# Score products in one order by shape, a third copy on ScalarE at the first change of tile, and eight buffers for modulation bias rows

## The chip, the cores and the metric

The kernel runs on one core of one Trainium2 chip. Its time is the device time of one execution in microseconds, as the median of a few runs. In the profile PE is the TensorE matmul, PEld its weight loads, DVE VectorE, ACT ScalarE, POOL GpSimd and SP SyncE; the DMA engines move data between memory (HBM) and the on-chip SBUF. Matmuls write into PSUM, which has eight banks of 512 float32 per partition.

## The reference

A trunk of two layers over 256 latent tokens and 256 context tokens, width 1024, all in float32. Each layer normalises, modulates, mixes, adds, and is followed by PEER, a mixer that picks 16 experts per head for each token:

```python
mod_x = split(silu(c) @ w_mod[i] + b_mod[i], 6)          # and mod_c from c_ctx
hx = rms_norm(x, norm1[i]) * (1 + mod_x[1]) + mod_x[0]
# layer 0: gated short convolution + bidirectional gated DeltaNet, layer 1: latent attention
x = x + mod_x[2] * mixer(hx)
hx2 = rms_norm(x, norm2[i]) * (1 + mod_x[4]) + mod_x[3]
x = x + mod_x[5] * peer(hx2)

def peer(hb):                  # for a tile of 128 tokens, 8 heads, 16 experts each
    s1, i1 = top_k(scores of half 0); s2, i2 = top_k(scores of half 1)
    sc, idx = top 16 of all sums s1 + s2
    gate = softmax(sc)
    act = gelu(einsum('td,thkd->thk', hb, u_tab[idx]))
    return einsum('thk,thkd->td', gate * act, v_tab[idx])

def attention(q, k, v):        # 8 heads, q and k are 128 plain + 64 rotary columns
    return softmax(q @ k.T * scale) @ v
```

## The kernel before

The program is written engine by engine: each engine has its own list of instructions in a fixed order, written out by hand, and waits for semaphores of the others. It has four blocks.

**First block (`first_block`, L1890).** The 24 chunks of modulation (2 layers, 12 chunks of 512 columns each) are computed by PE from 2 MB of weights each that SP loads (`mod_pe`, L1841). Chunks 0 to 3 come at the start, chunks 4 to 23 one after another inside the DeltaNet mixer of the context tokens, woven with its stages by `beside`. For chunk n DVE adds the bias (`mod_dve`, L1854), which POOL has loaded into `mod_row[n % 4]`, and for gains it multiplies with `norm_row[n % 4]`. The rows lie in `straight` (1024 columns, 128 for each) and `diag`, both unused by anything else in this block. POOL stores the result to memory, waits until the store before it has landed, and loads the bias of chunk n + 3 (loop at L1928). DVE's instructions of the mixer stand behind `mod_dve` in its order. In a mixer chunk PE computes KS, vT, QS, kT, then vnew, intraV and dS, and DVE takes them at L1130, L1135 and L1139, L1143, L1146, L1153, L1163, L1170 and L1173; then ACT squares the output (L977), and output product, norm, scores and ranking follow up to the first gather.

**Sums (`sums_and_mixer`, L2716; `last_sums`, L3228).** There are six tiles of 128 tokens (T_ 0 to 5, 8 heads each, head number G = 8 T_ + h). For each expert k of a head POOL gathers 128 rows of 8 KB (1 MB) into one of 9 slots (L2063), DVE forms the dot products with the first half (L2267), ACT makes gelu, coefficient and a diagonal matrix `diag` of two experts (L2079, L2080, L2085), and PE adds the second halves with eight 64x64 products (16 matmul records) into four banks of PSUM (L2185), which frees the two slots for POOL's next two gathers. Two of the four banks hold sums in place (straight), two hold the halves of partitions crossed over. Between these groups of two experts the rest of the kernel is woven in by stages; in tiles 0 and 1 that is the whole context-free half of layer 0 (its projections and mixer), with the same lines as in the first block. Where one tile ends, ACT copies the crossed halves into the tile's place (L2114), DVE adds the straight ones during the next head, after its fourth dot product (`SUM_AT`, L2120), and the place then holds the sum. Tiles 0 and 1 use the same four banks. PE waits before its first group of tile 1 (`tile_open_pe`, L2150) through

```python
        def sums_copied(pe, T_):
            pe.wait_ge(peer_crossed, 2 * T_ + 2)      # ACT's two copies
            pe.wait_ge(peer_straight, T_ + 1)         # DVE's add
```

**The pause (`second_block`, L2833).** After tile 3 no gather can run: the attention of layer 1 needs the last context tile. Attention of the latent tile 2 over the first three tiles of keys was computed earlier; here the scores against the last 128 keys (`st`, two banks, one for even and one for odd heads) are merged with it. PE's order is: keys; scores (L2994 with 128 rows, L2995 with 64 rotary rows, `rows_of(par)`); values (L2490, recorded at L1246); the turned probabilities (L3003); the rest of a projection (L1246); new outputs (L3013); turns (L3020); the output product (L1246). DVE takes each bank's maximum (L2921 to L2924), copies half of the values (`values_take`, L2926), rescales the earlier output (L2930 to L2934) and adds the new (L2938). ACT takes the exponentials (L2881, four for each bank), then the other half of the values (L2885).

A float32 product shows as two matmul records; a turn (a product with the identity) as one.

## Time and profile before

| | |
|---|---|
| median of 3 runs | 2475.72 us (2472.72 to 2481.14) |
| the profiled execution | 2469.39 us, its span 2467.6 us |
| mean granted TensorE clock | 0.859 of 2.4 GHz |
| PE, PEld busy | 1776.8 us (72%), 847.2 us (34%) |
| DVE, ACT, POOL busy | 1630.6 us (66%), 971.8 us (39%), 980.0 us (40%) |
| DMA | 938.60 MB, mean 380 GB/s |

The span goes from the first instruction to the last; 1.8 us of the profiled execution's time lie around it. All times in the rows are from the span's start. Busy shares are means over stages with different limits, so they do not tell what an edit is worth; the chain of waits does, which is followed back from the last instruction, at each step to what released it. In it "issue" is time in which an engine waited for nothing that the profile shows. In a timeline row the bracket gives the idle time before and who ended it; "x16" is the number of records merged in the row.

### The profile page before, as it was taken

The numbers are of one execution on the slowest core, as the hardware profiler recorded it, in microseconds if no ns is written. First come the engines' busy times: TensorE is split into PE (matmuls) and PEld (weight loads), VectorE is DVE, ScalarE is ACT, GpSimd is POOL, SyncE is SP. The second block draws the span as 40 slices with busy tenths as digits, with TensorE's granted clock in tenths as the row PEclk, the third lists the DMA queues.
The fourth block names the chain that finished last, engine by engine and source line by source line (L and its number), as shares of the span: only waits on it lengthen the run. The fifth ranks groups of instructions, "written<-read, shape, count | busy, mean of one in ns | idle before, by whom it ended". The sixth has DMA issues, their size and how long they took to land.

```text
span 2467.6 us, 35626 instructions
## 1 busy us (share of the span) xinstructions
PE 1776.8 (72%) x13118; PEld 847.2 (34%) x13118; DVE 1630.6 (66%) x3826; ACT 971.8 (39%) x2654; POOL 980.0 (40%) x896
## 2 busy tenths in 40 slices
PE   7998979997875869557665566766978765555555
PEld 5877656553542215112221122221643411111111
DVE  1544567969997676577666675775386666666665
ACT  3411147744434334235533353453254333433333
POOL 3014133344443334445544444443044444454452
PEclk9999999998998889768787887888998968787877
DMA  8278689999989999999999999998389999999997
GB/s 353 75 274 343 256 332 385 421 421 421 382 360 423 420 422 404 418 422 421 422 421 421 420 415 420 409 405 340 147 369 421 420 421 421 418 421 421 420 419 293
DMA packets 127967, 938.60 MB, mean 380 GB/s; under 512 B 17168, under 2 KB 18192, under 8 KB 20784
## 3 DMA queue, kind: packets, MB, share of 16 engines
q0 software_dynamic: 114800, 807.34, 79.3%
q1 hardware_dynamic: 12992, 128.97, 13.0%
q8 instruction: 104, 1.70, 0.3%
q14 instruction: 71, 0.58, 0.1%
HBM read 935.10 MB, written 1.15 MB: 379 GB/s over the span
## 4 chain that ended last, share of the span: by engine, by line
DMA 42%; PE 34%; DVE 11%; ACT 6%; issue 6%; POOL 1%; DVEq 0%; SPq 0%; ACTq 0%; POOLq 0%
DMA arena<-in_experts,expert_cur 37%; PE ps L2185 13%; PE ps L1246 12%; DVE arena L2267 5%; DMA last_slot<-in_experts,expert_cur 4%; ACT diag L2085 2%; PE ps L1850 2%; PE ps L1271 2%; PE ps L1258 1%; PE ps L1482 1%; ACT coef L2080 1%; PE ps L1463 1%; ACT acts L2079 1%; POOL arena L2063 1%; ACT L2079 1%
## 5 line engine op out<-in xcount | busy, mean ns | idle before, releaser
L2185 PE MATMUL ps<-arena,diag 64*64 64x512 f32 x5464 | 980.9, 767 | 554.8 <-ACT diag L2085 548.5
L2063 POOL DMA_INDIRECT arena<-in_experts,expert_cur x683 | 811.0, 1187 | 1142.5 <-PE ps L2185 909.5
L2267 DVE CUSTOM_DVE_ANT_0 arena<-arena 128x1024 f32<-128x1024 f32 x683 | 838.6, 1229 | 510.6 <-DMA arena<-in_experts,expert_cur 498.0
L2185 PEld LDWEIGHTS ps<-arena,diag 64*64 64x64 f32 x5464 | 237.3, 158 | 1126.9 <-ACT diag L2085 800.7
L2079 ACT ACTIVATE acts<-dots 128x2 f32<-128x2 f32 (+1 forms) x386 | 78.6, 204 | 1007.6 <-DVE dots L2267 993.3
L2085 ACT ACTIVATE diag<-consts,coef 128x128 f32<-128x128 f32 x768 | 266.4, 393 | 12.6
L2185 PE MATMUL ps<-last_slot,diag 64*64 64x512 f32 x680 | 211.4, 749 | 45.2 <-ACT diag L2085 45.1
L2080 ACT ACTIVATE coef<-acts,gate_cur 128x1 f32<-128x1 f32 x768 | 185.1, 288 | 12.6
L1246 PE MATMUL ps<-wring 128*128 128x256 f32 (+2 forms) x568 | 146.7, 410 | 0.0
L2267 DVE CUSTOM_DVE_ANT_0 last_slot<-last_slot,arena 128x1024 f32<-128x1024 f32 x85 | 104.4, 1228 | 55.0 <-DMA last_slot<-in_experts,expert_cur 53.6
L2063 POOL DMA_INDIRECT last_slot<-in_experts,expert_cur x85 | 100.6, 1183 | 92.2 <-PE ps L2185 77.0
L1246 PEld LDWEIGHTS ps<-wring 128*128 128x128 f32 x568 | 100.6, 197 | 63.6 <-issue 54.8
L1246 PE MATMUL ps<-arena,wring 128*128 128x256 f32 (+1 forms) x576 | 115.1, 357 | 0.1
L1246 PEld LDWEIGHTS ps<-arena,wring 128*128 128x128 f32 x576 | 98.9, 194 | 19.3 <-issue 8.2
L2079 ACT ACT_TABLE_LOAD x80 | 102.6, 1283 | 6.7 <-DVE dots L2267 5.3
L1869 POOL DMA_DIRECT2D mods<-straight x48 | 26.7, 558 | 166.7 <-DVEq L1864 159.3
L2185 PEld LDWEIGHTS ps<-last_slot,diag 64*64 64x64 f32 x680 | 51.2, 160 | 110.5 <-ACT diag L2085 72.5
L2267 DVE DVE_READ_ACCUMULATOR2_ANT dots<- 128x1 f32 x768 | 63.1, 82 | 0.0
L2091 ACT ACT_TABLE_LOAD x47 | 60.3, 1283 | 0.8
L1850 PE MATMUL ps<-wring,small 128*2 128x128 f32 x1152 | 38.3, 282 | 16.0 <-DMA wring<-in_w_mod 11.8
L1246 PE MATMUL ps<-arena 128*128 128x128 f32 (+2 forms) x190 | 44.8, 390 | 2.0 <-ACT arena L2469 0.8
L1258 PE MATMUL ps<-arena 128*128 128x128 f32 x352 | 45.0, 281 | 1.7 <-issue 1.7
(402 smaller groups left out, 1985.5 us busy)
## 6 DMA issues: line engine op xcount, KB each, us to landing
wring<-in_w_mod SPq DMA_DIRECT2D x18, 2048.0 KB, 9.8
wring<-in_ev_w_in SPq DMA_DIRECT2D x14, 1024.0 KB
arena<-in_w_mod SPq DMA_DIRECT2D x6, 2048.0 KB, 10.0
wring<-in_ev_w_in SPq DMA_DIRECT2D x6, 2048.0 KB, 13.9
arena<-in_experts,expert_cur POOLq DMA_INDIRECT x683
wring<-in_w_q SPq DMA_DIRECT2D x5, 2048.0 KB, 12.8
wring<-in_ev_w_out SPq DMA_DIRECT2D x3, 2048.0 KB, 12.6
arena<-in_ev_w_in SPq DMA_DIRECT2D x1, 2048.0 KB, 19.9
```

Of the source, the lines that this page charges most:

```text
L1246: ins = nc.tensor.matmul(dst, l, r, start=first and i == 0, stop=last and i == len(pairs) - 1)
L1258: last = (M(dst, lhsT(h), rhs(h), start=True, stop=True) if op is M else TR(dst, lhsT(h), rhs(h)))
L1271: last = M(dst, lhsT[c, u, :], rhs[c, u, :], start=True, stop=plus is None)
L1850: last = nc.tensor.matmul(ps[32 * g:32 * g + 2, 6 + n % 2, 0:P], sT[:, 2 * k:2 * k + 2], w[:, k, g, :], start=(k == 0), stop=(k == KT - 1))
L1869: pool.dma_start(quarters(mods[i, s, c // 2, (c % 2) * 512:(c % 2) * 512 + 512]), mod_row[n % 4][s:P:32]).then_inc(rows_stored[n % 2], 16)
L2063: nc.gpsimd.indirect_dma_start(ring_slot(slot), None, table, bass.IndirectOffsetOnAxis(ap=expert_cur[:, par, k:k + 1], axis=0),).then_inc( ...
L2079: act_step(nc.scalar.activation(acts[:, par, g], dots[:, par, g], ACT.Gelu))
L2080: act_step(*[nc.scalar.activation(coef[:, par, k:k + 1], acts[:, par, k:k + 1], ACT.Copy, scale=gate_cur[:, par, k:k + 1]) for k in ks])
L2085: nc.scalar.activation(diag[:, k % RING, :], const(IDENT), ACT.Copy, scale=coef[:, par, k:k + 1]).then_inc(diag_ready, 1)
L2091: nc.scalar.activation(gate_exp[:, :], best[:, :], ACT.Exp, bias=gate_stat[:, 0:1], accum_out=gate_stat[:, 1:2]).then_inc(gexp_ready, 1)
L2185: last = nc.tensor.matmul(ps[rows_of(o), sum_bank(G // PH, odd, c), :], diag[rows_of(i), k % RING, rows_of(i)], ring_slot(RING_SLOT[G, k]) ...
L2267: ins = nc.vector.tensor_tensor_reduce(out=ring_slot(slot)[:, 0:D], in0=ring_slot(slot)[:, 0:D], in1=place, scale=1.0, scalar=0.0, op0=ALU ...
```

## The change

Three edits. (1) `mod_row` and `norm_row` get eight entries instead of four. Four more stretches of `straight` and `diag` are zeroed, and the rows of chunks 4 to 7 are loaded behind the small constants, before the first store; the loop then loads chunk n + 7 after storing chunk n. (2) At the end of tile 0 alone, ACT also copies the straight sums, into `straight`; PE waits for ACT's three copies and no more for DVE, and DVE adds `straight` from SBUF. (3) In the pause, PE does the eight score products over 128 rows first, then the eight over 64 rows, alternating between the even and the odd bank and with that between the two halves of rows; DVE's copy of its half of the values moves behind the four small steps of the first bank.

```diff
+ROWS = 8
...
-        mod_row = [straight[:, P * k:P * k + P] for k in range(4)]
-        norm_row = [diag[:, k, :] for k in range(4)]
+        mod_row = [straight[:, P * k:P * k + P] for k in range(ROWS)]
+        norm_row = [diag[:, k, :] for k in range(ROWS)]
...
+        first_sums_kept = sem("first_tile_sums_copied")
...
         def mod_dve(dve, n):
             V = nc.vector
-            dve.wait_ge(row_landed[n % 4], 32 * sum(1 + is_gain(m) for m in range(n % 4, n + 1, 4)))
+            dve.wait_ge(row_landed[n % ROWS], 32 * sum(1 + is_gain(m) for m in range(n % ROWS, n + 1, ROWS)))
...
+                nc.gpsimd.memset(straight[:, N_COLUMNS * P:ROWS * P], 0.0).then_inc(rows_zero, 1)
+                nc.gpsimd.memset(diag[:, N_COLUMNS:ROWS, :], 0.0).then_inc(rows_zero, 1)
+                pool.wait_ge(rows_zero, 4)
+                for n in range(N_COLUMNS, ROWS):
+                    load_mod_rows(pool, n)
...
-                    if n and n + 3 < len(MODS):
+                    if n and n + ROWS - 1 < len(MODS):
                         if n <= N_COLUMNS:
                             pool.wait_ge(column_done, n)
-                        load_mod_rows(pool, n + 3)
+                        load_mod_rows(pool, n + ROWS - 1)
...
             for i in range(2):
                 nc.scalar.copy(by_banks(place)[rows_of(i)], crossed_sum(T_, i)).then_inc(peer_crossed, 1)
+            if T_ == 0:
+                nc.scalar.copy(by_banks(straight[:, :]), straight_sum(T_)).then_inc(first_sums_kept, 1)
...
             dve.wait_ge(peer_crossed, 2 * T_ + 2)
-            nc.vector.tensor_tensor(by_banks(place), by_banks(place), straight_sum(T_), ALU.add).then_inc(peer_straight, 1)
+            if T_ == 0:
+                dve.wait_ge(first_sums_kept, 1)
+                nc.vector.tensor_tensor(place, place, straight[:, :], ALU.add).then_inc(peer_straight, 1)
+            else:
+                nc.vector.tensor_tensor(by_banks(place), by_banks(place), straight_sum(T_), ALU.add).then_inc(peer_straight, 1)
...
             else:
-                sums_copied(pe, T_ - 1)
+                pe.wait_ge(peer_crossed, 2)
+                pe.wait_ge(first_sums_kept, 1)
...
-                values_take(dve, V.tensor_copy, 3, 1)
                 for par, c in enumerate(parity):
...
                     step(V.tensor_tensor(alpha_rec[:, c], alpha[:, c], all_rec[:, c], ALU.mult))
+                    if par == 0:
+                        values_take(dve, V.tensor_copy, 3, 1)
                     step(V.tensor_tensor(half_o[:, par], half_o[:, par], over(alpha_rec[:, c]), ALU.mult))
...
                 for par in range(2):
                     for i in range(4):
-                        at = slice(i * P, (i + 1) * P)
-                        M(banks[par][:, at], qnT[2][:, 2 * i + par, :], knT[:, 2 * i + par, new], start=True, stop=False)
-                        last = M(banks[par][:, at], qrT[2][rows_of(par), i, :], krT[rows_of(par), new], start=False, stop=True)
-                    product.mark(last, ("st", par))
+                        M(banks[par][:, quarter(i)], qnT[2][:, 2 * i + par, :], knT[:, 2 * i + par, new], start=i == 0,
+                          stop=False, skip_group_check=True)
+                for i in range(4):
+                    for par in range(2):
+                        last = M(banks[par][:, quarter(i)], qrT[2][rows_of(par), i, :], krT[rows_of(par), new], start=False,
+                                 stop=True, skip_group_check=True)
+                        if i == 3:
+                            product.mark(last, ("st", par))
```

## Rows read from the trace of the kernel before

**Rows 1.** The page: the chain that ended last, by engine.

```profile
DMA 42%; PE 34%; DVE 11%; ACT 6%; issue 6%; POOL 1%; DVEq 0%; SPq 0%; ACTq 0%; POOLq 0%
```

**Rows 2.** The chain of waits in the first block, 235 to 345 us: start, duration, what.

```profile
252.35 7.72 DMA mods<-straight
...
261.17 7.20 DMA straight<-in_b_mod
```

**Rows 3.** Timeline, 236 to 300 us: start, duration, engine, line, names, count, [idle before].

```profile
266.93 1.49 PE L1258 MATMUL ps<-arena 128*128 128x128 f32 x11 [0.86 <-issue]
...
268.40 0.29 DVE L1859 TENSOR_TENSOR straight<-ps,straight 128x128 f32<-128x128 f32 x1 [2.77 <-DMA straight<-in_b_mod]
...
269.13 5.65 PE L1258 MATMUL ps<-arena 128*128 128x128 f32 x48
...
273.17 1.29 DVE L1163 TENSOR_TENSOR arena<-arena,ps 128x512 f32<-128x512 f32 x2 [0.21 <-PE ps L1258]
...
275.82 1.28 DVE L1173 TENSOR_TENSOR arena<-arena,ps 128x512 f32<-128x512 f32 x2
```

**Rows 4.** Timeline of POOL alone, 0 to 64 us.

```profile
16.15 1.16 POOL L1869 DMA_DIRECT2D mods<-straight  x2 [4.16 <-DVEq L1864]
```

**Rows 5.** Timeline, 690 to 720 us, the first change of tile.

```profile
700.07 2.04 ACT L2114 COPY arena<-ps 64x1024 f32<-64x1024 f32 x2 [4.73 <-PE ps L2185]
...
702.88 0.69 ACT L2085 ACTIVATE diag<-consts,coef 128x128 f32<-128x128 f32 x2
...
707.89 1.15 DVE L2120 TENSOR_TENSOR arena<-arena,ps 128x1024 f32<-128x1024 f32 x1
...
709.14 3.69 PE L2185 MATMUL ps<-arena,diag 64*64 64x512 f32 x16 [4.00 <-issue]
...
713.12 0.94 POOL L2063 DMA_INDIRECT arena<-in_experts,expert_cur  x1 [10.64 <-PE ps L2185]
...
714.23 0.69 DVE L1163 TENSOR_TENSOR wring<-wring,ps 128x512 f32<-128x512 f32 x1 [1.33 <-PE ps L1258]
```

**Rows 6.** Stretches: PE, PEld, DVE, ACT, POOL busy us; granted clock; DMA share; GB/s.

```profile
706.00:722.00 16.00, 12.86 (x142) 7.82 (x143) 13.15 (x24) 5.93 (x15) 4.50 (x4) 0.79 0.60 222
708.00:714.00 6.00, 4.86 (x25) 2.12 (x26) 4.80 (x7) 4.66 (x11) 0.88 (x1) 0.56 0.22 89
720.00:731.00 11.00, 9.28 (x102) 5.94 (x96) 10.50 (x28) 5.28 (x18) 8.87 (x8) 1.00 0.89 324
731.00:750.00 19.00, 13.41 (x96) 5.92 (x96) 16.59 (x41) 4.62 (x18) 9.11 (x8) 0.91 1.01 423
```

**Rows 7.** Timeline of PE alone, 700 to 760 us.

```profile
723.28 1.95 PE L2185 MATMUL ps<-arena,diag 64*64 64x512 f32 x16 [0.22 <-ACT diag L2085]
```

**Rows 8.** Timeline, 1725 to 1790 us, the pause between the two layers' sums.

```profile
1735.67 3.84 PE L1246 MATMUL ps<-arena 128*128 128x128 f32 x32 [0.76 <-ACT arena L2469]
...
1740.81 0.46 PE L2994 MATMUL ps<-arena 128*128 128x128 f32 x2
...
1741.20 0.49 PE L2995 MATMUL ps<-late,arena 64*128 64x128 f32 x2
...
1745.47 0.37 ACT L2881 ACTIVATE arena<-ps,small 128x128 f32<-128x128 f32 x1 [7.12 <-DVEq L2925]
...
1747.45 3.70 PE L1246 MATMUL ps<-arena 128*128 128x512 f32 x8
...
1751.86 1.46 PE L1246 MATMUL ps<-wring,straight 128*128 128x384 f32 x4
...
1753.15 1.95 PE L3013 MATMUL ps<-x,arena 128*128 128x128 f32 x16
...
1754.85 2.16 DVE L2938 SCALAR_TENSOR_TENSOR arena<-ps,small,arena 128x128 f32<-128x128 f32 x8
```

**Rows 9.** Timeline, 1778 to 1830 us: products over 64 rows.

```profile
1784.06 0.72 PE L3067 MATMUL ps<-arena,consts 64*128 64x128 f32 x8 [0.51 <-issue]
...
1790.87 1.13 PE L2788 MATMUL ps<-late 64*128 64x512 f32 x4
```

More of the change, by code:

```diff
@@ L577, in build @@
         c_landed = sem("c_landed")
-        row_landed = [sem(f"mod_bias_landed{i}") for i in range(4)]
+        row_landed = [sem(f"mod_bias_landed{i}") for i in range(ROWS)]
         mod_done = sem("mod_chunk_done")
@@ L1855, in mod_dve @@
             V = nc.vector
-            dve.wait_ge(row_landed[n % 4], 32 * sum(1 + is_gain(m) for m in range(n % 4, n + 1, 4)))
+            dve.wait_ge(row_landed[n % ROWS], 32 * sum(1 + is_gain(m) for m in range(n % ROWS, n + 1, ROWS)))
             dve.wait_ge(mod_done, n + 1)
-            row = mod_row[n % 4]
+            row = mod_row[n % ROWS]
             V.tensor_tensor(row, ps[:, 6 + n % 2, 0:P], row, ALU.add).then_inc(mod_taken, 1)
@@ L1861, in mod_dve @@
             if is_gain(n):
-                dve_step(V.scalar_tensor_tensor(out=row, in0=row, scalar=1.0, in1=norm_row[n % 4], op0=ALU.add,
+                dve_step(V.scalar_tensor_tensor(out=row, in0=row, scalar=1.0, in1=norm_row[n % ROWS], op0=ALU.add,
                                                 op1=ALU.mult))
@@ L1869, in store_mod_rows @@
                 pool.dma_start(quarters(mods[i, s, c // 2, (c % 2) * 512:(c % 2) * 512 + 512]),
[L1870 removed]
+                               mod_row[n % ROWS][s:P:32]).then_inc(rows_stored[n % 2], 16)
         def column_pe(pe, n):
@@ L1919, in _ @@
                 pool.wait_ge(rows_zero, 2)
-                for n in range(4):
+                for n in range(N_COLUMNS):
                     load_mod_rows(pool, n)
```

10 lines of the change are left out of this document (5 added, 5 removed).

## The prediction

> **What bounds the kernel now.** I read the page first, then the chain of waits, then timelines of the three places that the change touches, then the table of stretches for the DMA engines. Over the whole span the chain is DMA 42% and PE 34% [rows 1]: the experts' rows come from memory at one rate for long stretches, and the waits between them are short pieces where another engine ends last. So an edit is worth what it takes out of one of those pieces, and I read each piece by itself. Three matter.
>
> First, the end of the first block. The chain passes through a store of modulation rows that takes 7.72 us to land and a load of bias rows of 7.20 us, one behind the other on POOL's queue [rows 2]; DVE stands 2.77 us for the last row's bias (L1859, 268.40) [rows 3]. Second, the first change of tile, near 705 us. ACT copies the crossed sums at 700.07 to 702.11 (L2114), but DVE comes to its add (L2120) only at 707.89, and PE, which must wait for both before it opens tile 1 in the same banks, stands idle 4.00 us until 709.14 [rows 5]. Its group then takes 3.69 us, and only then does POOL issue the next gather, at 713.12, having waited 10.64 us. Meanwhile the DMA engines run dry: their share is 0.60 over 706 to 722 us and 0.22 over 708 to 714, where the granted clock is 0.56, that is, mostly the lower of its two levels [rows 6]. From 731 us their share is 1.01. Third, the pause between the two layers' sums, 1720 to 1795 us, where no gather is in flight and PE, ACT and DVE follow each other in one serial chain.
>
> **Part 1, eight bias rows.** The last row's load (n = 23) is issued today when the store of row 19 has landed; with eight buffers it is issued at n = 16, seven chunks ahead, so DVE's 2.77 us goes. What is late next: DVE's L1143 needs the state product QS, whose matmuls PE does at 266.93 to 268.42 [rows 3], and PE does not wait for DVE there. Step by step: DVE does row 23 by 265.95, takes the first half of QS at 267.4 and the second at 268.45, ends at 269.1 (1.0 us ahead of now), then L1146 and L1153 at their own 1.28 and 1.4 us to 271.9. L1163 needs intraV; PE's 48 matmuls from 269.13 take 5.65 us whatever DVE does, and intraV is their second third, done about 272.9. The second L1163 then ends at 273.7, the two L1170 at 275.1 and L1173 at 276.4, against 275.82 + 1.28 = 277.10. So 2.77 us of wait are worth 0.7 us. Bounds: 0, if PE's own order holds all of it; 1.6, if PE's pause of 0.86 us inside QS goes too. All behind it (squares, output product, ranking, first gather) is serial, so 0.7 us stays. The costs: two more memsets and eight more loads on POOL, about 8 x 0.56 + 1.0 = 5.5 us, in a hole of 4.16 us before the first store [rows 4]; that store goes 1.4 us later and nobody waits for it (the columns are turned on PE from SBUF, and what it frees is loaded for a chunk that comes more than 100 us later). Without that cover it would be at most 5.5 us. I take 0.
>
> **Part 2, ACT copies the straight sums too, at the first change only.** ACT's third copy writes 128x1024; the copies of 64x1024 take 1.0 us each [rows 5] and time goes by elements per partition, so 1.05 us, to 703.15. ACT's queue behind it: gelu, coefficients and the diagonals of head 8, which end now at 703.57, then at 704.6; two copies of vnew, later by 1.0 but needed by PE only after its group. PE finishes the woven work at 709.14 - 4.00 = 705.14, later than all of these, so it opens tile 1 at 705.2: 3.9 us earlier. It has not stood idle, so I take its group at 1.95 us, as the group at 723.28 [rows 7] in a stretch whose granted clock is 1.00, that is 2.4 GHz [rows 6], not 3.69. The slots are free at 707.15 and POOL issues at 707.4 instead of 713.12: 5.7 us earlier. The next pair of slots is freed after PE's woven intraV and level products (4 us), at about 713 instead of 718.9, the pair after that when DVE's dots and ACT allow, at 716.5. So the DMA engines, with two gathers of 1 MB at 2.5 us each, stay fed: of the 16 x (1 - 0.60) = 6.4 us idle in 706 to 722 about 2 remain, 4.4 gained.
>
> DVE sets the other limit. Its add still stands at 707.89, both operands in SBUF now, at the same price; so DVE gains only its waits for PE, 1.33 us at 714.23 and some 0.6 at the two level products behind it, 2.0 in all. In 731 to 750 us DVE is busy 16.59 of 19 us [rows 6], so it can catch up 2.4 us more as its data comes sooner: 4.4 again. From there DMA's share is 1.01, which keeps what it has gained. I take 4.4. Bounds: 2.0 (DVE never catches up, and the gathers queue behind it) and 5.7 (the whole advance of the first gather); 0 is excluded as long as PE's 4.00 us goes.
>
> **Part 3, the pause's scores.** Now 8 products over 128 rows and 8 over 64 alternate, each two matmul records, from 1740.81 to 1747.45: 6.64 us for 32 records, 0.21 each. The key products just before have the same 128x128 shape at the same clock and take 3.84 us for 32, 0.12 each [rows 8]. So the alternation costs almost as much again. After: 16 records at 0.12 make 1.9 us. For the 64-row ones the two nearest rows are 0.72 us for 8 records, which are not alternated between row halves, and 1.13 us for 4 of 512 columns, which are [rows 9]; the first gives 1.4 us for 16 records, the second, at a quarter of the columns, 1.13. I take 1.4: 3.3 us in all, 3.3 less. If a change of row half cost as much as a change of shape does now, they would stay at 0.21: 3.4 us, and the gain would be 1.4. The Trainium skill, "TensorEngine Tiling (Array Packing)", section Key Properties, says that a change of tiling mode, not of tile alone, drains the engine. By that rule the alternation is what costs, and the new order, with one change instead of fifteen, keeps the 3.3 us; the trace agrees that the alternation is dear, 0.21 against 0.12, and cannot show the rest, as no row has 128-column products that change row half.
>
> What is late next: st 1 is now ready at 1744.1, not 1747.5, but st 0 too, and it was ready at 1744.2 before; so ACT's first four exponentials begin at 1745.4 as now (1745.47) [rows 8] and take about 1.6 us. The second four follow at once, at 1747.1, and end at 1748.7. PE does the two value products meanwhile, 3.70 us to 1747.8, turns the probabilities by 1749.05, does the rest of the query latent (1.46) to 1750.5 and the new outputs (1.95) to 1752.4. DVE's values copy, moved behind the first half's four small steps, fills a time in which it waits for the second alpha; in its old place it would hold the first half behind the value product, so moving it costs nothing and keeps DVE ahead of PE: both half_o multiplications end by 1750.9. L2938 (eight, 2.16 us) starts at 1751.5, is held once by PE, and ends at 1753.7 instead of 1757.01. The output product, which waits for it, then starts 3.3 us earlier, and that is kept whole, since what follows to the first gather is serial. Its last weights are asked for at 1750.5 and first needed some 5 us later. Bounds: 1.0 (ACT's second set is the only thing that moves) and 3.9.
>
> **The sum.** 0.7 + 4.4 + 3.3 = 8.4 us, with bounds 3.0 and 11.2. The profiled execution took 2469.39 us, the span 2467.6 and 1.8 around it; it would be 2461.0. The median of the runs shown is 6.3 us above it, so for the median I say 2475.7 - 8.4 = 2467.3. A measurement here can tell about 0.3%, 7.4 us, from no change, so the forecast lies just beyond that line.
>
> **The rivals.** (a) DVE keeps the tile change's gain down. For it: DVE is busy 10.50 of 11 us in 720 to 731 [rows 6], and its own gain there is only 2.0 us; against it, 2.4 us are free in the 19 us behind. Then 0.7 + 2.0 + 3.3 = 6.0 us, 2469.7. (b) The 64-row products remain slow because they alternate row halves; the chain then gains 1.4 us instead of 3.3: 6.5 us in all, 2469.2. For it: nothing in the trace has 128-column products alternating so; against: the pair of 512 columns overlaps, 1.13 us for what two such would take alone. (c) The refill of 705 us does not count: DMA was only early, and later holes are as long. Then 4.0 us, 2471.7; against it is the share of 1.01 behind. (d) Slower: the earlier gathers change which woven products meet which head, PE stands idle longer before some groups, and those run at the lower clock, 3.69 us instead of 1.95 [rows 5, 7], 1.7 us each on the chain. Five such groups cancel the gain; ten make the kernel slower by more than 0.3%, 2484. For it, groups at the lower clock occur all over the sums; against, the DMA queue is full there and hides them. (e) The row buffers do nothing, because PE holds DVE anyway: 7.7 us, 2468.0.
>
> **How the numbers follow.** Forecast, with (e), 0.56; (a) 0.18; (b) 0.10; (c) 0.10; (d) 0.06. The forecast's own range is 2464 to 2470. The range for 8 in 10 leaves out most of (d) and the far end where all bounds are met together: from 2475.7 - 11.2, taken on to 2462 because the three runs shown differ by 8.4 us and their median is loose by a few, up to 2475. More than 0.3% faster (below 2468.3): 0.75 of the forecast case, 0.42, and 0.06 from (a) and (b): 0.48. Slower by more than 0.3%: half of (d) and a little for what I don't see, 0.05. The rest, 0.47, within 0.3%.
>
> **What would show it.** In the profile after: no wait for the bias rows on DVE in the first block, the squares (L977) 0.7 us earlier; PE's group at 705.2 less what came before, at 1.95 us, DMA share over the 16 us behind it near 0.9, and the same lead still there at 800 us; score products in 3.3 us, the output product 3.3 us earlier against the pause's start. I am wrong if PE's pause at 705 is only moved to another wait, if the lead at 800 us is under 3 us, if the 64-row products take 0.2 us each, or if stretches between the three places change length by more than a microsecond or two.

## The result, and the profile after

The changed kernel takes 2463.0 us (median of 6 executions, 2457.4 to 2467.3), the kernel before 2474.8 us (6 executions beside them, 2472.7 to 2481.1). The ratio is 0.9948, with an interval of 0.9932 to 0.9964: 12.9 us faster, 8.9 to 16.8. The forecast was 2467.3 us and a gain of 8.4 us. The direction was right, and the predicted gain is just outside the interval. One execution each of pause_halves, no_rows, tile_waits, tile_twice and rows_twice, 2538 to 8531 us long, is left out of all that follows.

The profiled execution took 2467.28 us, 2.1 us less than that of before and the longest of its six. So the two profiles set side by side hide most of the gain, and each stretch has to be read by its own length, not by its place on the clock.

**The first block.** The timeline of the changed kernel, 262 to 290 us, answers to [rows 3]:

```profile
269.48 1.93 PE L1852 MATMUL ps<-wring,small 128*2 128x128 f32 x64
...
271.34 0.82 PE L1260 MATMUL ps<-arena 128*128 128x128 f32 x5
...
271.63 0.28 DVE L1861 TENSOR_TENSOR straight<-ps,straight 128x128 f32<-128x128 f32 x1
...
273.29 1.49 PE L1260 MATMUL ps<-arena 128*128 128x128 f32 x11 [1.13 <-issue]
...
273.93 0.69 DVE L1145 TENSOR_TENSOR arena<-ps,small 128x512 f32<-128x512 f32 x1 [2.01 <-PE ps L1260]
...
281.51 1.29 DVE L1175 TENSOR_TENSOR arena<-arena,ps 128x512 f32<-128x512 f32 x2
```

The last bias row (L1861, which was L1859) no longer waits for anything. The next instruction, L1145, waits 2.01 us in its place, for PE's product QS, and PE itself pauses 1.13 us in the middle of that product with no wait recorded. The wait has changed its name and kept most of its length. PE's products for the last chunk start here at 269.48, and in the kernel before at

```profile
263.39 1.93 PE L1850 MATMUL ps<-wring,small 128*2 128x128 f32 x64
```

From there DVE needs 12.03 us to its last step of the mixer (L1175) where it needed 12.43 (L1173), so 0.4 us is gained on this piece, and PE comes to it 6.1 us later.

**The first change of tile.** The timeline of the changed kernel, 698 to 730 us, answers to [rows 5]:

```profile
707.10 2.04 ACT L2121 COPY arena<-ps 64x1024 f32<-64x1024 f32 x2 [4.69 <-PE ps L2199]
...
709.16 1.01 ACT L2123 COPY straight<-ps 128x1024 f32<-128x1024 f32 x1
...
712.02 1.91 PE L2199 MATMUL ps<-arena,diag 64*64 64x512 f32 x14
...
714.22 0.94 POOL L2070 DMA_INDIRECT arena<-in_experts,expert_cur  x1 [4.67 <-PE ps L2199]
...
714.96 1.15 DVE L2131 TENSOR_TENSOR arena<-arena,straight 128x1024 f32<-128x1024 f32 x1
```

ACT's third copy takes 1.01 us. PE opens the second tile at 711.91 without an idle gap, its 16 products take 2.0 us instead of 3.69, and DVE's add comes only after them. POOL waits 4.67 us for its slot instead of 10.64. The stretches of the changed kernel, with the columns of [rows 6]:

```profile
706.00:722.00 16.00, 12.11 (x179) 8.16 (x174) 14.84 (x27) 11.49 (x25) 6.05 (x6) 1.00 1.02 402
708.00:714.00 6.00, 4.96 (x65) 3.62 (x66) 5.19 (x10) 4.86 (x11) 1.24 (x2) 1.00 1.00 416
713.00:729.00 16.00, 12.03 (x163) 7.65 (x158) 15.07 (x29) 7.43 (x21) 6.17 (x6) 1.00 0.99 384
731.00:750.00 19.00, 13.71 (x104) 6.63 (x96) 18.57 (x49) 5.46 (x20) 10.65 (x10) 0.91 0.98 392
```

ACT's copies start 7.0 us later here than in the kernel before (707.10 and 700.07), so the stretch that answers to its 706 to 722 us is 713 to 729. The DMA engines' share there is 0.99 where it was 0.60, and the granted clock is 1.00 from 706 to 729 us, where 708 to 714 us of the kernel before had 0.56.

**The pause.** The timeline of the changed kernel, 1740 to 1760 us, answers to [rows 8]:

```profile
1742.82 2.02 PE L3009 MATMUL ps<-arena 128*128 128x128 f32 x16
1744.77 1.16 PE L3013 MATMUL ps<-late,arena 64*128 64x128 f32 x16
1745.86 3.70 PE L1248 MATMUL ps<-arena 128*128 128x512 f32 x8
...
1747.21 0.37 ACT L2895 ACTIVATE arena<-ps,small 128x128 f32<-128x128 f32 x1 [6.85 <-DVEq L2939]
...
1750.75 1.46 PE L1248 MATMUL ps<-wring,straight 128*128 128x384 f32 x4
...
1753.21 2.16 DVE L2953 SCALAR_TENSOR_TENSOR arena<-ps,small,arena 128x128 f32<-128x128 f32 x8 [0.68 <-PE ps L3033]
...
1755.92 4.53 PE L1248 MATMUL ps<-wring,arena 128*128 128x512 f32 x10
```

The 32 records of the scores take 1745.86 - 1742.82 = 3.04 us instead of 6.64. The output product, the last row, starts 13.10 us after the first score; in the kernel before that was 16.84 us.

### The profile page after: what moved, and what is told of

Read it like the earlier page. It is cut to its first block, busy times and chain, and to the rows that moved or that the text cites. A ratio compares the mean times of both kernels' runs of the same rounds, so it can differ in the third digit from the quotient of the medians.

```text
span 2465.5 us, 35630 instructions
## 1 busy us (share of the span) xinstructions
PE 1780.7 (72%) x13118; PEld 850.7 (35%) x13118; DVE 1631.1 (66%) x3826; ACT 972.8 (39%) x2655; POOL 966.9 (39%) x898
## 3 DMA queue, kind: packets, MB, share of 16 engines
q1 hardware_dynamic: 12992, 128.97, 13.2%
## 4 chain that ended last, share of the span: by engine, by line
DMA 41%; PE 36%; DVE 11%; issue 6%; ACT 5%; POOL 0%; DVEq 0%; SPq 0%; POOLq 0%; ACTq 0%
DMA arena<-in_experts,expert_cur 36%; PE ps L2199 13%; PE ps L1248 12%; DMA last_slot<-in_experts,expert_cur 4%; DVE arena L2281 4%; ACT diag L2092 2%; PE ps L1852 2%; PE ps L1260 2%; PE ps L1273 2%; PE ps L1484 1%; ACT coef L2087 1%; PE ps L1465 1%; ACT acts L2086 1%; PE ps L1890 1%; DVE last_slot L2281 0%
## 5 line engine op out<-in xcount | busy, mean ns | idle before, releaser
L2070 POOL DMA_INDIRECT arena<-in_experts,expert_cur x683 | 793.2, 1161 | 1144.0 <-PE ps L2199 913.6
L2087 ACT ACTIVATE coef<-acts,gate_cur 128x1 f32<-128x1 f32 x768 | 185.1, 288 | 12.6
L1852 PE MATMUL ps<-wring,small 128*2 128x128 f32 x1152 | 38.1, 281 | 16.1 <-DMA wring<-in_w_mod 11.7
L1248 PE MATMUL ps<-wring,arena 128*128 128x512 f32 x102 | 45.6, 599 | 0.0
## 6 DMA issues: line engine op xcount, KB each, us to landing
arena<-in_w_mod SPq DMA_DIRECT2D x6, 2048.0 KB, 10.4
```

The costliest lines, as they stand in the source:

```text
L1248: ins = nc.tensor.matmul(dst, l, r, start=first and i == 0, stop=last and i == len(pairs) - 1)
L1852: last = nc.tensor.matmul(ps[32 * g:32 * g + 2, 6 + n % 2, 0:P], sT[:, 2 * k:2 * k + 2], w[:, k, g, :], start=(k == 0), stop=(k == KT - 1))
L2070: nc.gpsimd.indirect_dma_start(ring_slot(slot), None, table, bass.IndirectOffsetOnAxis(ap=expert_cur[:, par, k:k + 1], axis=0),).then_inc( ...
L2087: act_step(*[nc.scalar.activation(coef[:, par, k:k + 1], acts[:, par, k:k + 1], ACT.Copy, scale=gate_cur[:, par, k:k + 1]) for k in ks])
```

## How the runs are compared

One execution of any of these kernels scatters by 2.5 to 5.6 us (standard deviation of the executions of one kernel), as much as the effects in question. Two measures are used beside each other. The first is the ratio of the times. The second is the length of a stretch in the profiled execution, between marks that every kernel has: the first dot product (DVE, L2267) of head 8, of head 20, of head 31 and of head 32 (heads counted from 0 through all the sums), and in the pause from the first score to the output product. A stretch is far steadier than a whole execution. The table has all 18 profiles. Its columns are: start to first dot of head 8; head 8 to head 20, which holds the change of tile; head 31 to head 32, which holds the pause; first score to output product; DVE's waits for bias or norm rows behind 60 us, in sum; PE's pauses with no recorded wait between 100 and 280 us, in sum. A letter shows what the kernel has: T the tile edit, O the new order of the scores, V the move of the values copy, R the eight row buffers.

```
                        to 8    8-20  31-32  scores  bias   PE pauses
before                 695.6   526.7  127.0  16.84    2.8   13.5
before_again           703.1   528.5  125.7  16.74    3.1   16.2
rows_lag               701.7   527.0  127.0  16.75    3.2   15.2
values_only      V     702.6   528.1  126.4  16.22    5.1   16.1
tile_waits      (T)    697.5   526.9  126.3  16.83    9.1   12.8
rows_only        R     699.5   525.0  126.9  16.74    0     18.2
rows_twice       R     699.5   527.2  126.9  16.74    0     15.0
pause_only       OV    699.5   527.6  122.1  13.20    1.3   14.7
order_only       O     699.3   527.0  122.1  13.15   10.4   12.4
pause_halves    (O)V   697.9   527.6  122.3  13.18    1.5   15.7
tile_only        T     702.1   522.1  126.0  16.74    3.2   12.2
tile_twice       T     700.4   522.2  127.0  16.75   14.6   12.9
tile_and_order   TO    704.0   523.4  122.4  13.14    8.3   15.1
both_twice       TO    698.8   522.2  122.3  13.15    6.0   13.2
no_rows          TOV   698.6   520.8  123.3  13.11    4.8   12.6
after            TOVR  702.7   522.3  122.2  13.10    0     17.7
after_again      TOVR  701.8   523.2  122.3  13.10    0     18.6
after_third      TOVR  701.5   523.1  122.3  13.10    0     14.9
```

And the times. The difference is that of the means against the executions of the kernel before on the same chip, with twice its standard error:

```
                 executions  ratio [interval]            difference, us
rows_only            12      1.0001 [0.9991, 1.0011]     +0.4 +- 1.9
rows_twice           11      0.9997 [0.9988, 1.0006]     -0.8 +- 2.0
rows_lag             11      1.0004 [0.9992, 1.0016]     +0.7 +- 2.1
before_again         11      0.9995 [0.9985, 1.0006]     -0.8 +- 2.2
tile_waits           11      0.9994 [0.9982, 1.0007]     -1.9 +- 2.4
values_only          12      0.9994 [0.9981, 1.0006]     -1.2 +- 2.8
tile_only            12      0.9981 [0.9969, 0.9993]     -3.7 +- 2.7
tile_twice           11      0.9982 [0.9965, 0.9998]     -5.2 +- 3.7
pause_only           12      0.9984 [0.9974, 0.9995]     -3.9 +- 2.0
order_only           12      0.9978 [0.9966, 0.9989]     -5.5 +- 2.3
pause_halves         11      0.9978 [0.9966, 0.9991]     -5.5 +- 2.6
tile_and_order        8      0.9960 [0.9946, 0.9974]     -9.6 +- 2.8
both_twice            6      0.9953 [0.9936, 0.9969]    -11.7 +- 3.7
no_rows               5      0.9955 [0.9940, 0.9970]    -11.1 +- 2.5
after                 6      0.9948 [0.9932, 0.9964]    -13.0 +- 4.0
after_again           6      0.9950 [0.9931, 0.9968]    -10.6 +- 4.2
after_third           7      0.9947 [0.9929, 0.9966]    -12.6 +- 4.1
```

## The experiments

**The whole again, and each part alone.** after_again is the changed kernel without an edit. rows_only takes from the change (shown above) all that has `ROWS` or `N_COLUMNS` in it and nothing else; tile_only takes the third copy, the add from SBUF and PE's new waits; pause_only takes the order of the scores and the place of the values copy.

> The changed kernel once more, for a second profile. Theory 1: the changed kernel's first profile was 5 to 9 us late before the first change of tile because PE paused by chance inside groups of the first block; then this profile reaches the first gather at another time, anywhere from 5 us earlier to the same, while the stretches at the change of tile (heads 8 to 11, minus 6.4 us in the first profile) and in the pause (minus 4.8 us) come out the same within 1 us. Theory 2: the eight row buffers cause the lateness; then the first gather is again 7 to 9 us later than in the kernel before.

> The eight row buffers alone. Prediction's step: minus 0.7 us, bounds 0 and minus 1.6; no wait for bias rows on DVE at the end of the first block. Rival: the buffers cost time in the first block, plus 5 to 9 us as in the first profile of the changed kernel. Second rival: they are worth more than priced, minus 2.8 us, the whole wait.

> ScalarE's third copy at the first change of tile alone. Prediction's step: minus 4.4 us. The first profile of the changed kernel says minus 6.4 us between the start of head 8 and the start of head 11. If DVE sets the limit (rival a) it is minus 2.0; if the refill does not count (rival c) 0. DMA share over the 16 us behind the change of tile 0.9 instead of 0.60.

> The pause's two edits alone (score order and DVE's values copy). Prediction's step: minus 3.3 us; the first profile of the changed kernel says minus 3.7 us up to the output product and minus 4.8 us from head 31 to head 32. If the 64-row products were slow (rival b) it is minus 1.4. Score products 3.1 us in all instead of 6.64.

Measured: 0.9950 for the whole, 1.0001 for the rows, 0.9981 for the tile edit, 0.9984 for the pause. So two parts gain and one does nothing. The parts add up to 7.2 us (mean differences), the whole gave 10.6 here and 13.0 in the first comparison; this gap is what later runs were for.

**The pause taken apart.** Three kernels. order_only has the new order and leaves the values copy where it was:

```diff
                 for par in range(2):
                     for i in range(4):
-                        at = slice(i * P, (i + 1) * P)
-                        M(banks[par][:, at], qnT[2][:, 2 * i + par, :], knT[:, 2 * i + par, new], start=True, stop=False)
-                        last = M(banks[par][:, at], qrT[2][rows_of(par), i, :], krT[rows_of(par), new], start=False, stop=True)
-                    product.mark(last, ("st", par))
+                        M(banks[par][:, quarter(i)], qnT[2][:, 2 * i + par, :], knT[:, 2 * i + par, new], start=i == 0,
+                          stop=False, skip_group_check=True)
+                for i in range(4):
+                    for par in range(2):
+                        last = M(banks[par][:, quarter(i)], qrT[2][rows_of(par), i, :], krT[rows_of(par), new], start=False,
+                                 stop=True, skip_group_check=True)
+                        if i == 3:
+                            product.mark(last, ("st", par))
```

values_only has just the move:

```diff
-                values_take(dve, V.tensor_copy, 3, 1)
                 for par, c in enumerate(parity):
...
                     step(V.tensor_tensor(alpha_rec[:, c], alpha[:, c], all_rec[:, c], ALU.mult))
+                    if par == 0:
+                        values_take(dve, V.tensor_copy, 3, 1)
```

pause_halves has both, but does the products over 64 rows half by half:

```diff
-                for i in range(4):
-                    for par in range(2):
+                for par in range(2):
+                    for i in range(4):
                         last = M(banks[par][:, quarter(i)], qrT[2][rows_of(par), i, :], krT[rows_of(par), new], start=False,
                                  stop=True, skip_group_check=True)
```

> The kernel before with the new order of the pause's scores alone: eight products over 128 rows first, then eight over 64 rows that alternate row halves; DVE's copy of the values stays at its old place, ahead of the first half's steps. Theory A (the forecast's): the scores take about 3.2 us instead of 6.64, but the values copy, which waits for PE's value product, holds DVE's first half until about 1751; so of the 3.3 us at most 2.5 reach the output product, and the time is about 2 to 2.5 us under the kernel before. Theory B (the copy's place does not matter, because PE is behind DVE there anyway): the whole 3.5 to 4 us, as with both edits of the pause together.

> The kernel before with only DVE's copy of the values moved behind the first half's four small steps; the scores stay alternated between 128 and 64 rows. Theory A (the forecast's: moving it costs nothing and gains only together with the new order): the output product starts within 0.3 us of where it does in the kernel before, counted from the first score; time the same. Theory B (the copy held DVE and through it the end already before): the output product starts 1 us or more earlier, and part of the pause's 3.74 us belongs to this edit.

> Both edits of the pause, but the eight products over 64 rows are done one row half after the other (four, then four) instead of alternating halves. It tells what the alternation of halves is worth. If alternating halves overlap: the 16 records take about 1.4 to 1.9 us here (0.09 to 0.12 each, as products that do not alternate) against 1.16 us (0.07 each) in the changed kernel, and the first half's scores are ready earlier by about half of it. If the alternation does nothing: 1.16 us here too. By either the output product starts 3 to 3.8 us earlier than before, and the time is 3 to 4 us under the kernel before; 0.21 each would say that the price before was that of 64 rows as such and not of the change of shape.

From the first score to the output product the kernels without the new order need 16.74 to 16.84 us, values_only 16.22, order_only 13.15, both edits 13.10 to 13.20. So the order alone brings 3.6 us, the move alone 0.5 us, and beside the new order the move brings 0.05 us at most. The forecast had the copy in its old place hold DVE's first half behind the value product; it does hold it (in order_only DVE's first step on alpha stands behind the copy, at 7.4 us after the first score), but PE's new outputs begin 9.2 us after the first score with or without the move, and L2938 then 10.4 us after it. Theory B was right for the order; for the move alone neither was, since it gains 0.5 us.

The timeline of pause_halves shows what the alternation of row halves is worth:

```profile
1742.95 2.02 PE L2995 MATMUL ps<-arena 128*128 128x128 f32 x16
1744.91 1.71 PE L2999 MATMUL ps<-late,arena 64*128 64x128 f32 x16
1746.10 0.69 DVE L2921 TENSOR_REDUCE small<-ps 128x4 f32<-128x512 f32 x1 [3.71 <-PE ps L2999]
...
1746.55 3.70 PE L1246 MATMUL ps<-arena 128*128 128x512 f32 x8
...
1756.13 2.38 PE L1246 MATMUL ps<-wring,arena 128*128 128x512 f32 x5
```

The 16 records take 1.71 us, 0.11 each, as products over 128 rows do, against 1.16 us, 0.07 each, when they alternate. Yet the output product comes 13.18 us after the first score here too: half by half, the first half's scores are ready early (DVE starts 0.45 us ahead of the value product, not 0.10 behind its start), and the chain behind, DVE, ACT and the turned probabilities, starts from there. The overlap of the halves is real and worth nothing on this path. The two PSUM banks alternate together with the row halves, so the runs do not tell which of the two lets the products overlap. What made the old order slow was the change between 128 and 64 rows, not the 64 rows: both new orders have one change and lose the 0.21 per record. They also set the two products of one quarter of a bank apart, but that is not it: the key products write each quarter twice in a row, too, and take 0.12 us per record [rows 8].

**Does the tile edit gain by PE's early opening?** tile_waits has the third copy and the add from SBUF, but PE waits for DVE's add again:

```diff
             else:
-                pe.wait_ge(peer_crossed, 2)
-                pe.wait_ge(first_sums_kept, 1)
+                sums_copied(pe, T_ - 1)
```

> The tile edit alone, but PE waits once more for VectorE's add before it opens the second tile; ScalarE's third copy and the add with both operands in SBUF stay. Theory A (the gain is PE's early opening, and through it the early gathers): the four gathers behind 705 us are asked for as late as in the kernel before, the stretch from the first dot of head 8 to that of head 12 stays near 185 us (184.2 in the kernel before, about 179 to 181 with the tile edit), and the time is within 1 us of the kernel before, 0 to 1 us worse for the third copy. Theory B (the add or ScalarE's copy itself pays): 2 us or more of the tile edit's 4 to 5 us remain.

The timeline of tile_waits:

```profile
711.04 3.69 PE L2192 MATMUL ps<-arena,diag 64*64 64x512 f32 x16 [4.00 <-issue]
...
715.03 0.94 POOL L2064 DMA_INDIRECT arena<-in_experts,expert_cur  x1 [10.66 <-PE ps L2192]
```

and its stretch:

```profile
706.00:722.00 16.00, 11.99 (x156) 7.65 (x159) 12.76 (x22) 6.89 (x17) 2.37 (x3) 0.79 0.63 246
```

With this one wait back, everything is back: PE's 4.00 us idle, the group at 3.69 us, POOL's 10.66 us, the DMA share of 0.63, and 526.9 us from head 8 to head 20, against 526.7 in the kernel before and 522.2 with the whole edit. The time is within 0.1% of before. Neither the copy nor the cheaper place of the add pays; the gain is PE's early opening and the gathers that follow from it.

**Without the rows, the two gaining edits alone, and repeats.** no_rows is the change without the eight buffers, tile_and_order the tile edit and the new order alone; tile_twice and after_third are tile_only and the changed kernel once more.

> The whole change without the eight bias row buffers: the tile edit and both edits of the pause. The parts by themselves gave 0.0 (rows), -4.7 (tile) and -4.0 us (pause), 8.6 in sum, where the whole gave about 12. Theory A (the parts add up, the whole's excess is scatter of executions): about -8.7 us, ratio 0.9965. Theory B (the row buffers pay only together with the rest, by 3 us or more): about -8.7 here too, but clearly less than the whole, and the whole stays at -12. Theory C (tile and pause strengthen each other, the rows do nothing): about -12 here, ratio 0.995.

> The two edits that have shown a gain, the tile edit and the new order of the scores, without the eight row buffers and without the move of the values copy. If the other two do nothing, it is as fast as the whole change: 9 us under the kernel before if the parts add up, 11 to 13 if tile and pause together give more than apart. If the move of the values copy matters in combination, its output product comes more than 0.3 us later after the first score than the 13.1 us of the changed kernel.

> The tile edit alone once more, for more executions beside the other kernels of this call. By the places in the traces it is worth about 4.9 us (head 8 to head 20), by the first 12 executions 3.7 to 4.7. If the parts add up, it is 4 to 5 us under the kernel before here too. If it is 6 us or more, the difference between the whole (11 to 13) and the sum of the parts (8.5) was this part's scatter.

> The changed kernel once more, beside its parts on one chip. If the whole is the sum of the parts by their places in the traces (tile 4.9, pause 4.2, rows 0): 9 us under the kernel before, ratio 0.9963. If parts strengthen each other: 11 to 13 us, ratio 0.995. If the row buffers cost or give something beside the other two, it differs from the run without them and without the values move by more than 2 us.

no_rows gave 11.1 us, tile_and_order 9.6, the tile edit alone 5.2 and the whole 12.6. All four are compatible with a sum of parts near 9 and with a whole near 11; two edits of the four carry what is gained.

**The rows.** In the first profiles every kernel with eight buffers had longer pauses of PE in the first block, above all one of about 2 us at 163 us, and no wait for bias rows. rows_lag keeps the buffers and their memsets and loads each row as late as before:

```diff
-                for n in range(N_COLUMNS, ROWS):
-                    load_mod_rows(pool, n)
...
-                    if n and n + ROWS - 1 < len(MODS):
+                    if n and n + 3 < len(MODS):
                         if n <= N_COLUMNS:
                             pool.wait_ge(column_done, n)
-                        load_mod_rows(pool, n + ROWS - 1)
+                        load_mod_rows(pool, n + 3)
```

> Eight row buffers and the two further memsets, but each row is loaded as late as in the kernel before (three chunks ahead). Theory A (the forecast's bookkeeping: only how early the loads are issued counts): VectorE's waits for bias rows are back (1 to 5 of them, 1 to 15 us in sum, as in the kernels with four buffers), and PE's pauses without a recorded wait between 60 and 330 us, 12 to 15 us in sum in kernels with four buffers and 15 to 18.5 us with eight, are 12 to 15 again. Theory B (the longer pauses come with the added instructions or buffers as such, or are chance): the pause of 1.8 to 2.1 us at 163 us is there though the loads are late. The time is within 0.1% of the kernel before by both.

> The row buffers alone once more. The profiles so far say: no wait of VectorE for a bias row, PE's pauses 15 to 18.5 us instead of 12 to 15, the last row's step no earlier. If the edit is worth the 0.7 us that was forecast, that can't be told from nothing here; if the longer pauses reach the end, the time is 1 to 3 us over the kernel before; the first 12 executions said +0.4 with an uncertainty of 1.

> The kernel before under another label: what the comparison says where nothing is changed. Ratio 1.000 with an interval of 0.001 to each side; its profile gives one more place of the first gather and of PE's pauses with four buffers (12 to 15 us in sum between 60 and 330 us, none over 1.5 us ahead of 166 us).

> The tile edit and the new order of the scores once more. The parts measured apart give 4.3 (tile, 23 executions) and 4.9 us (order with or without the values copy, 35 executions), 9.2 in sum; this pair gave 9.6, the pair with the values copy 11.1, the whole change 10.6 to 13. If the parts add up, this run lies 8 to 11 us under the kernel before; under 12 us or more would say that the two strengthen each other.

The pause at 163 us does not need the edit. The timeline of PE in before_again, in which no part of the change is:

```profile
163.94 0.56 PE L1271 MATMUL ps<-arena 64*64 64x64 f32 x11 [2.11 <-issue]
```

It has the 2 us pause, and 16.2 us of pauses; rows_twice, with eight buffers, has no such pause there, and 15.0 us in sum. rows_lag has the waits for bias rows back, as bookkeeping says, and a pause of 1.79 us at 163.1. So long pauses come without the edit. Whether the early loads lengthen them besides stays open. The 13 profiles with loads as late as before have 12.2 to 16.2 us of pauses, mean 14.0, the five with early loads 14.9 to 18.6, mean 16.9; of all ways to choose five of these 18 profiles, 0.3% give a difference of 2.9 us or more, which speaks for the edit. In the four profiles of this last round there is none: 15.0 us with early loads, and 15.2, 16.2 and 13.2 without. In the times nothing is seen.

What the early loads do is plain in all five: DVE never waits for a row, and from the last row's step to L1170 it takes 7.3 to 8.4 us instead of 6.0 to 7.2, because it now waits for PE. Counted from PE's first product for the last chunk to the end of L1173, it takes 12.2 to 13.3 us instead of 13.3 to 16.8, so DVE is nearer behind PE. But PE comes to that product at 267.8 us on average with early loads and at 264.5 without, and its pauses make 3.0 of the 3.3 us. Head 8 starts at 701.0 us on average with them and at 700.1 without.

both_twice gave 11.7 us, before_again 0.8: an unchanged kernel can look 0.8 us faster.

## Why the prediction had the mechanisms right and the gain too small

**The step that failed is the sum.** The forecast added three pieces, 0.7 + 4.4 + 3.3 = 8.4 us, and put all that lies outside them at nothing. The first comparison measured 12.9 us, over the forecast's own upper bound of 11.2, and the six comparisons of kernels with both gaining edits 11.2 +- 1.4 together. Inside the sum the terms for the tile (4.4, measured 4.8) and the pause (3.3, measured 3.6) were too small by 0.7 us together, and the term for the rows (0.7, nothing seen) was too large by about as much. What the profiles show behind the first dot of head 8 is 8.8 us. The other 2 to 4 us (2.4 of 11.2, 4.1 of 12.9) lie in no term, and their cause stays open.

**Part 1, the rows: forecast 0.7 us; the times of rows_only and rows_twice together say 0.2 +- 1.4 us faster.** The mechanism was forecast and is there: the row's wait goes, PE's QS is late next, and the piece from PE's last chunk to the end of L1173, 13.7 us in the kernel before and 13.0 by the forecast, takes 12.2 to 13.3. What no run shows is the step behind it, that all the rest is serial and so the 0.7 us stays. That step took the place at which PE comes to its last chunk from one execution as fixed; with early loads it came there 3.3 us later on average, by its longer pauses, which may be chance or a price of the edit. A value of 0, the lower bound and rival (e), fits the times, and so does 0.7. The two added memsets are in rows_lag too, whose time is 0.7 +- 2.1 us over the kernel before.

**Part 2, the tile: forecast 4.4 us, measured 4.8 in the traces.** That is the difference of the means from head 8 to head 20: 522.4 in 8 profiles with the edit (520.8 to 523.4), 527.2 in 10 without (525.0 to 528.5). In the times it is 3.7 and 5.2 us. Each step held: the third copy 1.01 us (forecast 1.05), PE at once behind its woven work, the group at 1.9 to 2.0 us (1.95), the DMA share up (0.9 forecast, 0.99 measured). POOL issues the next gather 7.1 us after ACT's first copy instead of 13.1, 5.9 us earlier (5.7 forecast). The lead is 5.6 us at head 11, near 835 us, 4.8 at head 20 and 4.4 at head 31. Rival (a), that DVE limits it to 2.0, fell: DVE was busy 18.57 of the 19 us in 731 to 750 (and again in 738 to 757), so it had the room to catch up that the forecast gave it and used it. Rival (c), that the refill does not count, fell by the same numbers, and rival (d), more groups at the lower clock, shows nowhere: from head 20 to head 31 every profile takes 453.3 to 454.3 us, 454.0 on average with the edit and 453.6 without, so 0.4 us at most is given back there.

**Part 3, the pause: forecast 3.3 us, measured 3.6.** The products over 128 rows take 2.02 us (1.9 forecast) and those over 64 rows 1.16 (1.4 forecast), less 0.14 by which they overlap each other and the value product behind. The term was sized by the row of 64-row products that do not alternate [rows 9], which is also what pause_halves shows (0.11 each); the alternating row of 512 columns, which gave 1.13, was the better guide. Rival (b), that the alternating halves stay at 0.21, fell. Of the steps behind, one was wrong without a cost: the values copy in its old place does not hold up the end. The rule of the Trainium skill, "TensorEngine Tiling (Array Packing)", Key Properties, that a change of tiling mode drains the engine and a change of tile alone does not, agrees with the scores: 0.21 us per record where 128 and 64 rows alternate, 0.07 where the row halves alone do. No run shows a drain as such.

**The sum.** By the traces 4.8 + 3.6 + 0 = 8.4 us. That the sum is the forecast's own is luck: two small errors against a third. There is a further difference from head 31 to head 32: 126.6 us in the 9 profiles without the new order, 122.3 in the 9 with it, 4.2 us. The 0.6 us over the 3.6 lies ahead of the scores, in the retiring of the last head, where a profile has either about 64.0 or about 65.1 us: the shorter in 8 of 9 with the new order and in 3 of 9 (before_again is one). An edit behind that stretch can't be shown to act on it, so this looks like chance; counted in, the traces say 9.0. Taken in one piece, from the first dot of head 8 to the end of the span, it is 1763.5 us in the six profiles with both edits (1762.8 to 1764.3) and 1772.3 in the seven with neither (1770.8 to 1773.7): 8.8 us.

**Why the whole measured more.** The six kernels that have both gaining edits are 9.6 to 13.0 us faster; their mean, weighted by their errors, is 11.2 +- 1.4 (some are compared with the same executions of the kernel before, so these errors are a little too small). The parts measured apart are 4.2 +- 2.2 for the tile (two kernels) and 4.8 +- 1.3 for the pause (three), 9.0 +- 2.5. So the forecast of 8.4 lies 2.8 us under the mean of the whole, and the parts and the traces account for 9.0 of it. The remaining 2 us are in no stretch that the profiles show: the profiles with both edits reach head 8 at 701.2 us on average, those with neither at 699.9, which is the wrong sign, and from head 32 to the last dot all are within 0.8 us of each other. As the time behind head 8 hardly scatters, what one execution has over another lies, by these profiles, in the first 700 us. The six profiled executions with both edits were 3.0 us slower than the means of their kernels, so the profiles may just have missed what made the others fast. That the edits strengthen each other isn't shown; what is left is within the errors of both sums, and stays open. One sign of being wrong that the forecast named did show in its pair of profiles: the stretch to head 8, outside all three places, grew by 7.1 us. Over all 18 profiles it is 695.6 to 704.0 us, whatever the edit. The forecast's median of 2467.3 us was also set on a base of 2475.7, 0.9 over the one measured beside the changed kernel.

The lesson of size is in the range, not in a term: no term was off by more than 0.7 us, but a median of six executions that scatter by 4 us is itself loose by 2, and the low end of the range, 2462 us, left just 1 us for it.

## What to carry to other kernels

Ask of a wait that is removed what the waiting engine needs next, and from whom; where the answer is an engine that runs without slack and pauses for unequal times, as PE in the first block here, a longer lead of the loads may buy little; here it bought nothing that the times can show (0.2 +- 1.4 us). A bank handed over between two engines is worth more than the copy that frees it: 1.0 us of copying on an idle ACT took away 4.0 us of PE's idle time and through it a gap in a DMA stream that set the end, and one wait put back took it all away again. Group small products by how many rows they use; the change between 128 and 64 rows cost here about as much as the product itself.

## What was not expected of the hardware

**PE pauses inside a group of products with no wait on record.** There are 10 to 14 such pauses between 100 and 280 us in every profile, 0.15 to 3.6 us each and 12 to 18.6 us in sum. The chain of waits of the changed kernel gives them as issue:

```profile
217.45 0.54 PE ps L1852 x13
217.98 2.58 issue
220.56 1.69 PE ps L1852 x51
```

Their places are fixed and only their lengths differ. The 213 pauses of the 18 profiles stand before only 19 records of PE's program, and neighbours among these 19 are 125 to 128 matmul records apart, each record with its weight load. The same place, which has a pause in all 18 profiles, has 0.85 us in one and 3.59 in another. So where a pause can stand goes by the position in PE's list of instructions. In no profile does one stand between 100 and 160 us. There the DMA engines' share is 0.53 at most in the kernel before, while between 160 and 260 us, where 10 of its 11 pauses stand, it is 0.81 to 1.00:

```profile
140.00:160.00 20.00, 20.00 (x226) 11.30 (x223) 5.12 (x14) 3.67 (x5) 0.00 (x0) 1.00 0.42 149
180.00:200.00 20.00, 14.40 (x378) 12.43 (x378) 7.17 (x15) 2.96 (x5) 7.59 (x14) 0.91 0.84 320
```

What fills the pauses no run here shows.

**The same products at two speeds by chance.** Between the first block's residual and the first ranking, eight products of 128 columns and four of 256 take 1.09 and 1.03 us in the kernel before, and 1.96 and 1.88 us in the profile of the changed one:

```profile
317.53 1.96 PE L841 MATMUL ps<-consts,arena 128*128 128x128 f32 x8 [2.23 <-DVE arena L830]
319.28 1.88 PE L1296 MATMUL ps<-arena 128*128 128x256 f32 x4
```

after_again, the same program, has the first of them as short as the kernel before:

```profile
316.47 1.09 PE L841 MATMUL ps<-consts,arena 128*128 128x128 f32 x8 [2.23 <-DVE arena L830]
```

The granted clock over 317 to 322 us of the changed kernel's profile is 0.66, so part of these products ran at the lower of the two levels, after the engine had been idle for 2.23 us; in the kernel before it is 1.00 over 311 to 316 us, after an idle time of 2.22 us. In after_again the clock fell later: it is 0.68 over 316 to 321 us, and the four products of 256 columns take 1.53 us. The stretch from L1170 to the first dot of head 0 has two lengths in all kernels, 55.4 to 56.4 us in 12 profiles and 58.4 to 59.7 in 6, and the 6 are just those whose first group takes 1.69 us or more (1.09 to 1.27 in the 12). From the start of the first group to PE's next products it is 3.46 us in the changed kernel's profile and 2.02 in that of before, 1.4 of the 3 us; up to that start all 18 agree within 0.02 us. It is one of the things that make one execution a poor witness of a change of 0.3%.

**Products over 64 rows that alternate row halves, and banks with them, overlap:** 0.07 us per record of 128 columns against 0.11 without alternation.
